# Sums of squares of queries and keys, from high and low parts in two one-pass matmuls

## The reference, cut to what matters

```
h = rms_norm(x, norm1_g)                       # x is 512 frames x 1024
z = h @ w_in
q = z[..., 512:1024].reshape(B, S, 8, 64)      # 8 heads of 64 channels
k = z[..., 1024:1536].reshape(B, S, 8, 64)
q = rms_norm(q, q_norm_g)                      # q * rsqrt(mean(q*q over 64) + 1e-6) * g
k = rms_norm(k, k_norm_g)
y_attn = forgetting_attention(q, k, v, log_f)
```

## Time and profile before

| what | us |
|---|---|
| median of 3 runs | 1446.62 (1446.37 to 1447.86) |
| the profiled execution | 1446.98 |
| its span (first to last instruction) | 1445.2 |
| PE busy | 1436.3 (99%) |
| DVE busy | 1121.8 (78%) |
| POOL busy | 976.9 (68%) |
| ACT busy | 570.5 (39%) |

### The profile page before, as it was taken

One profiled execution on the slowest core, in us unless ns is written; L12 is line 12 of the kernel. 1 busy time (PEld: TensorE's weight loads), 2 busy tenths in 40 slices (PEclk: granted clock), 3 DMA queues, 4 the chain that ended last, 5 costly groups with the idle time before them and its releaser, 6 DMA issues.

```text
span 1445.2 us, 20413 instructions
## 1 busy us (share of the span) xinstructions
PE 1436.3 (99%) x7551; PEld 1277.5 (88%) x7551; DVE 1121.8 (78%) x1868; ACT 570.5 (39%) x790; POOL 976.9 (68%) x535
## 2 busy tenths in 40 slices
PE   9999999999999999999999999999999999999998
PEld 6766788899999999999999999888888888888887
DVE  5668661569999999699999995587767777777775
ACT  5665353333333333444444444333333333333332
POOL 4432434436778878866666665588887888878883
PEclk9999999999999999999999999999999999999999
DMA  5321223235787888989999985998888888888883
GB/s 210 119 74 59 90 107 117 74 102 171 246 276 259 263 276 276 339 284 358 363 355 362 365 306 195 399 397 323 339 346 344 341 315 344 346 345 328 328 303 118
DMA packets 122437, 381.57 MB, mean 264 GB/s; under 512 B 11784, under 2 KB 28424, under 8 KB 122384
## 3 DMA queue, kind: packets, MB, share of 16 engines
q1 hardware_dynamic: 70528, 202.69, 39.6%
q0 software_dynamic: 36864, 134.23, 25.4%
q10 hardware_dynamic: 14992, 44.06, 7.8%
HBM read 336.89 MB, written 44.06 MB: 264 GB/s over the span
## 4 chain that ended last, share of the span: by engine, by line
PE 95%; DVE 1%; DMA 1%; ACT 1%; POOL 0%; issue 0%; SPq 0%; DVEq 0%; ACTq 0%
PE bank L718 28%; PE bank L720 28%; PE bank L719 28%; PE bank L954 6%; PE bank L886 1%; DMA raw<-v_dram 1%; PE bank L834 1%; PE wide L846 0%; PE bank L734 0%; PE bank L857 0%; DMA raw<-wst_dram 0%; PE wide L718 0%; PE wide L719 0%; PE wide L720 0%; DVE pad L1158 0%
## 5 line engine op out<-in xcount | busy, mean ns | idle before, releaser
L469 POOL TENSOR_TENSOR wl<-raw,wh 128x1024 fp32r<-128x1024 f32 x209 | 509.8, 2441 | 277.0 <-ACT wh L499 275.0
L718 PE MATMUL bank<-hh,wh 128*128 128x384 f32 (+1 forms) x1184 | 416.3, 352 | 0.2 <-DVE hl L1174 0.2
L719 PE MATMUL bank<-hl,wh 128*128 128x384 f32 (+1 forms) x1184 | 406.5, 343 | 0.0
L720 PE MATMUL bank<-hh,wl 128*128 128x384 f32 (+1 forms) x1184 | 406.4, 343 | 0.0
L718 PE MATMUL bank<-wh,Wh 128*128 128x512 f32 x768 | 298.9, 389 | 1.3 <-DVE Wl L1381 1.3
L720 PE MATMUL bank<-wh,Wl 128*128 128x512 f32 x768 | 298.8, 389 | 0.0
L719 PE MATMUL bank<-wl,Wh 128*128 128x512 f32 x768 | 298.8, 389 | 0.0
L499 ACT ACTIVATE wh<-raw 128x1024 fp32r<-128x1024 f32 (+1 forms) x217 | 228.4, 1053 | 148.1 <-PE bank L720 137.5
L718 PEld LDWEIGHTS bank<-hh,wh 128*128 128x128 f32 x1184 | 222.8, 188 | 7.9 <-DVE hl L1174 0.6
L719 PEld LDWEIGHTS bank<-hl,wh 128*128 128x128 f32 x1184 | 222.8, 188 | 7.1 <-issue 0.2
L720 PEld LDWEIGHTS bank<-hh,wl 128*128 128x128 f32 x1184 | 222.3, 188 | 7.6
(11 more groups left out here) (190 smaller groups left out, 1626.5 us busy)
## 6 DMA issues: line engine op xcount, KB each, us to landing
raw<-uT_dram SPq DMA_DIRECT2D x128, 512.0 KB, 4.3
xraw<-v_dram SPq DMA_DIRECT2D x72, 512.0 KB, 9.3
raw<-v_dram SPq DMA_DIRECT2D x56, 512.0 KB, 9.1
a_dram<-act_a ACTq DMA_DIRECT2D x64, 384.0 KB, 5.8
wf<-a_dram SPq DMA_DIRECT2D x32, 768.0 KB, 6.9
raw<-wst_dram SPq DMA_DIRECT2D x40, 512.0 KB, 3.3
gates_dram<-gbuf ACTq DMA_DIRECT2D x32, 512.0 KB, 6.9
gt<-gates_dram SPq DMA_DIRECT2D x32, 512.0 KB, 4.0
```

The source lines that it names most:

```text
L469: pool.tensor_tensor(wl[:, n % SPLIT, :], raw_of(n), wh[:, n % SPLIT, :].bitcast(F32), ALU.subtract).then_inc(w_lo, 1)
L718: pe.matmul(dst, ah, bh, start=start, stop=False)
L719: pe.matmul(dst, ah, bl, start=False, stop=False)
L720: return pe.matmul(dst, al, bh, start=False, stop=stop)
```

## The change

The fp32 matmul of `sum_square` becomes two fp32r matmuls into the same bank: one with the high part of the squares, one with the low part. The matrix of ones is copied once to an fp32r tile `blockr` by ACT (ones and zeros are the same in both types). The parts come from a new job `"parts"`: ACT copies the squares to `sq_high`, DVE subtracts that from the squares into `sq_low`. There is one buffer of each. In the table, `"parts"` is put into the stage of its sum: at step 3 for sums 0 and 1, at step 0 for the others; the sum itself moves from step 4 to step 5 for sums 0 and 1, from step 1 to step 2 for sums 3, 5 and 7, and stays at step 2 for sums 2, 4 and 6. The `sq` ring has three slots, not four.

```diff
-        sq = sb("sq", [P, 4, T], where=mixers)
+        sq = sb("sq", [P, 3, T], where=mixers)
+        sq_high = sb("sq_high", [P, T], F32R, mixers)
+        sq_low = sb("sq_low", [P, T], F32R, mixers)
+        blockr = sb("blockr", [P, P], F32R, mixers)
...
-            norm_b = [(1, "ss", 2 * c + 3), (4, "norm", 2 * c + 3)] if c < 3 else [(1, "poolmix", 1), (7, "mean", 2)]
+            norm_b = [(2, "ss", 2 * c + 3), (4, "norm", 2 * c + 3)] if c < 3 else [(1, "poolmix", 1), (7, "mean", 2)]
...
-            return [("proj", n, sorted(one + norm_a + last, key=lambda item: item[0])),
-                    ("proj", n + 1, sorted(two + norm_b, key=lambda item: item[0]))]
+            parts = [[(0, "parts", z)] if c < 3 else [] for z in (2 * c + 2, 2 * c + 3)]
+            return [("proj", n, sorted(parts[0] + one + norm_a + last, key=lambda item: item[0])),
+                    ("proj", n + 1, sorted(parts[1] + two + norm_b, key=lambda item: item[0]))]
...
-            return [(4, "ss", i), (5, "norm", i)]
+            return [(3, "parts", i), (5, "ss", i), (6, "norm", i)]
...
             def square(i, src):
-                if i >= 4:
-                    act.wait_ge(sq_used, i - 3)
-                act.activation(sq[:, i % 4, :], src, ACT.Square).then_inc(sq_ready, 1)
+                if i >= 3:
+                    act.wait_ge(sq_used, i - 2)
+                act.activation(sq[:, i % 3, :], src, ACT.Square).then_inc(sq_ready, 1)
...
                     if kind(n) == "f":
+                        act.wait_ge(in_consts, 16)
+                        act.activation(blockr[:, :], block_ones, ACT.Copy).then_inc(blockr_ready, 1)
...
+                elif what == "parts":
+                    act.wait_ge(sq_ready, SQ_QK + i + 1)
+                    act.wait_ge(sq_used, SQ_QK + i)
+                    act.activation(sq_high[:, :], sq[:, (SQ_QK + i) % 3, :], ACT.Copy).then_inc(sq_hi, 1)
...
-            def sum_square(i, weights, start, stop):
-                pe.wait_ge(sq_ready, i + 1)
-                pe.matmul(bank[SS][:, :], weights, sq[:, i % 4, :], start=start, stop=stop).then_inc(sq_used, 1)
+            def sum_square(i):
+
+                pe.wait_ge(blockr_ready, 1)
+                pe.wait_ge(sq_lo, i + 1)
+                pe.matmul(bank[SS][:, :], blockr[:, :], sq_high[:, :], start=True, stop=False)
+                pe.matmul(bank[SS][:, :], blockr[:, :], sq_low[:, :], start=False, stop=True)\
+                  .then_inc(sq_used, 1)
...
+                elif what == "parts":
+                    dve.wait_ge(sq_hi, i + 1)
+                    dve.tensor_tensor(sq_low[:, :], sq[:, (SQ_QK + i) % 3, :],
+                                      sq_high[:, :].bitcast(F32), ALU.subtract).then_inc(sq_lo, 1)
```

More of the change, by code:

```diff
@@ L211, in program @@
         w_hi, w_lo, w_used, pool_split = sem("w_hi"), sem("w_lo"), sem("w_used"), sem("pool_split")
+        blockr_ready, sq_hi, sq_lo = sem("blockr_ready"), sem("sq_hi"), sem("sq_lo")
         sq_ready, sq_used, ss_done = sem("sq_ready"), sem("sq_used"), sem("ss_done")
@@ L813, in run @@
                         pe.wait_ge(zc_used, i)
-                    sum_square(SQ_QK + i, block_ones, True, True)
+                    sum_square(i)
                 elif what == "poolmix":
@@ L1040, in add_square @@
                 if k == 1:
-                    dve.tensor_tensor(bank[SS][:, :], sq[:, (i - 1) % 4, :], sq[:, i % 4, :], ALU.add).then_inc(sq_used, 2)
+                    dve.tensor_tensor(bank[SS][:, :], sq[:, (i - 1) % 3, :], sq[:, i % 3, :], ALU.add).then_inc(sq_used, 2)
                 elif k:
                     dve.wait_ge(sq_used, i)
-                    dve.tensor_tensor(newt[:, :] if k == KD - 1 else bank[SS][:, :], bank[SS][:, :], sq[:, i % 4, :],
+                    dve.tensor_tensor(newt[:, :] if k == KD - 1 else bank[SS][:, :], bank[SS][:, :], sq[:, i % 3, :],
                                       ALU.add).then_inc(sq_used, 1)
```

## The result

The changed kernel takes 1457.55 us (median of 6 runs, 1456.64 to 1458.05) where the kernel before takes 1447.53 (6 runs, 1446.37 to 1449.34): ratio 1.007, 95% interval 1.0059 to 1.008, so 10.0 us slower. The forecast was 9.1 us slower, 1455.7. The profiled execution took 1457.79 us with a span of 1456.0, 10.8 more than the 1445.2 of before.

What follows compares the result with a forecast made beforehand. PE, busy 99% of the span and holding 95% of the chain, was taken as the bound. Waits of 12.38 us less savings of 3.28 gave +9.1 us, 1455.7 us; range 1451.5 to 1460.0.

Steps and rivals of the forecast that it cites:

- The bound: Whole kernel: PE, busy 99% of the span, bounds it; a microsecond of PE work or idleness moves the end by one.
- The saving, 0.41 a sum: At each of eight sums, two fp32r matmuls cost 0.46 us instead of 0.87; 3.28 us in all.
- the third slot costs nothing: The `sq` ring: a square now waits for the sum three back, done long before, so no cost.
- The hold by POOL: Sums 0 and 2: a subtraction starting inside POOL's L469 ends 0.55 us behind it, instead of taking 0.69 us.
- Rival 1: Subtractions at sums 0 and 2 not held by POOL: only +5.7 us, 1452.3; chance 14%.
- The queues at each sum: Work queued ahead of copy and subtraction makes PE wait 4.33, 3.08, 2.97, 1.87, 0.67 us at sums 0, 1, 2, 3, 5.
- Sum 1 and the clock: Sum 1: subtraction just clear of POOL, sum starts at 58.42, PE waits 3.08 us; clock stays full.
- The clock full between 44 and 82 us: Sign expected in the profile after: PE's granted clock stays full over that stretch despite the waits.
- rival 2: PE's clock halves behind the long wait at sum 0: 1458.1 us, or 1460.5 if again at sum 2; chance 12%.
- the upper bound named for sum 1: Subtraction 1 could also meet POOL's L469 of stage 9: 1 to 2 us more, +11 in all.
- My price of 2.4 us: Cost of a halved clock over the 24 matmuls up to sum 1: 11.0 us against about 8.6.

Runs made afterwards that it cites:

- e1: Kernel before, each sum as two one-pass matmuls at the old places, the second of zeros, low parts left out: 1444.0 us, ratio 0.9979.
- e5: Kernel before with three slots of squares and the sums at the change's later steps, still one fp32 matmul: 1446.67 us, ratio 0.9993.
- e2: Changed kernel with POOL's L474 held until the subtractions of sums 0, 1 and 2 are done: 1454.69 us, ratio 1.0049.
- e8: Changed kernel with 4, 3, 3 and 1 fp32 matmuls of zeros filling PE's waits ahead of sums 0 to 3: 1456.97 us, ratio 1.0061.
- e9: Changed kernel with POOL waiting for subtractions 0 to 2 and 2, 3, 1, 1 matmuls of zeros ahead of sums 0 to 3: 1455.65 us, ratio 1.0048.
- e10: As e9, but DVE scales the four value tiles behind subtraction 1, with no filler matmuls at sum 1: 1450.72 us, ratio 1.0021.
- e7: As e6, but parts of squares 3, 5 and 7 made behind their stage's second scores, those sums a step later: 1444.43 us, ratio 0.9977.
- e4: Changed kernel still making both parts, but PE sums the squares in one fp32 matmul without waiting for parts: 1453.1 us, ratio 1.0037.
- e6: Changed kernel with copies and subtractions made earlier in ACT's and DVE's queues, most values scaled later, some sums moved: 1445.01 us, ratio 0.9983.
- e3: Changed kernel with four fp32 matmuls of zeros filling PE's wait ahead of sum 0 only: 1458.71 us, ratio 1.0075.

## Why the prediction was right, and where not

- **The bound.** Right: what PE waited more it lost at the end. e1 saves 3.3 us on PE and ends 3.5 earlier; in the changed kernel PE's waits, its slow stretch and the saving make 10.3 of the 10.8 us.
- **The saving, 0.41 a sum.** Right: 3.3 forecast, 3.5 measured (e1). That the third slot costs nothing is right too (e5).
- **The hold by POOL.** Right: 2.41 and 2.35 us at sums 0 and 2, 0.69 without POOL beside it (e2). Rival 1 (no hold) said 3.4 us less; removing it brought 2.9 in the medians of e2, with the clock still falling, and 3.44 between the traces of e8 and e9.
- **The queues at each sum.** Right at sums 2, 3 and 5 within 0.25 us of wait, and at 4, 6 and 7, where none came. The parts are late because of what stands ahead of them: four values at sum 1 (e10), weights and POOL at sum 0 (e7).
- **Sum 1 and the clock.** Here the steps failed. "The clock full between 44 and 82 us" was wrong; rival 2, which had 12%, is part of what happened. The wait at sum 1 was 1.58 and not 2.9, since PE came late, at half its clock, into a wait that was longer than its loss. What counts is that the sum itself came 1.20 us later: 0.58 for the add behind a slow pair, 0.62 for a subtraction that now met POOL, the upper bound named for sum 1. My price of 2.4 us was too high: it put all 24 matmuls between the sums at half clock, and only the pair and ten more ran so; of their 2.5 us 1.3 lay in a wait that was there anyway. That the sum came so near without the clock is in part luck: the forecast had nothing in it that made the fall cheap.
- **What the forecast did not see.** It priced the parts through PE's wait for `sq_low` alone. e4 shows 5.7 us with no such wait, through DVE's queue. In the changed kernel the sum over that wait came out right, since the add stands behind the same subtraction either way. But of the kernel without the wait I expected 0 to 1.5 us, and it lost 5.7.
- **Open.** Of the 10.8 us between the two spans, 0.3 are not placed by the sums' starts (0.2 of them lie between sums 5 and 7, where PE won 0.63 and not 0.82), 0.5 by PE's account. The prices from traces rest on one profiled execution of each kernel. Whether the clock falls is not told by the length of a wait alone: see below.

## What to carry to other kernels

Where one engine is busy 99% of the time, a cheaper instruction on it is worth its saving only if its new inputs are there when it comes to them: read what stands ahead of them in each queue at that place, and who stands behind them too. Make such inputs right behind their source and ahead of work that nobody waits for soon, and keep DVE's instructions with two SBUF inputs away from POOL's; here that turned 10 us lost into 3 us gained. Two events inside one trace (sum 0 to sum 5) measure a term of a microsecond better than medians that differ in their first waits: e9's median hid 2 of its 3.4 us.

## What the runs showed of the hardware

- A DVE instruction with two SBUF inputs that starts inside a POOL one of 128x1024 ends 0.54 to 0.56 us behind it: 2.41, 2.35 and 1.31 us in the changed kernel, 1.40, 1.27 and 1.27 in e6, 2.47 in e4, against 0.69 alone, however far into POOL's 2.4 us it started (up to 1.66, in e6). With one input in PSUM it is not held (in e6 L1109 took 0.70 us inside L474). The order decides: where the subtraction started 0.38 us ahead of L474 (e6, 52.03 and 52.41), it kept its 0.69, and L474 took 2.58 instead of 2.40.
- PE's clock fell to 1.2 GHz at waits of 4.10 (changed kernel), 2.99 and 2.74 (e3), 2.34 and 2.06 (e2) and 2.29 us (e9), and at 0.30 and 1.31 us close together (e5). It stayed full at waits of 2.74 (changed kernel, granted 1.00 from 70 to 82 us), 2.54 (e4), 1.58, 1.47 and 1.32 (before). So the same length is found on both sides. The fall can come inside the wait (changed kernel, 4.10) or over a microsecond behind it (e3, 2.99: the first matmul there still takes 0.47 us). It did not fall where matmuls of zeros filled the waits (e8).
- Of the 2.5 us that half the clock cost PE, 1.1 to 1.2 reached the end: the rest fell into its next wait, and part of it came through ACT and POOL, whose late work met a subtraction.
